# Radius-64 scores against 256 keys at once, and an output projection dealt out between the others

## What is computed

```python
proj = rms_norm(x, norm_g[0]) @ a_w_in              # 512 x 1024 by 1024 x 10240
for g, (window, dil) in enumerate(((128, 1), (512, 4), (2048, 16))):
    q, k, v = (part of proj for group g)            # 8 heads of 128
    s = q @ k.T * 128**-0.5 - slope * distance      # |distance| <= window / 2, multiples of dil
    o[g], lse[g] = softmax(s) @ v, logsumexp(s)
w = softmax(lse over g)
y = sum(w[g] * o[g]) * silu(gate)
x = x + y @ a_w_out                                 # 1024 x 1024
```

## Time and profile before

| what | value |
|---|---|
| runs | median 1941.76 us of 3 (1941.34 to 1943.03) |
| profiled execution | 1942.72 us, span 1940.9 us |
| PE busy over the span | 1800.2 us (93%) |
| DVE busy | 1084.6 us (56%) |
| ACT busy | 732.9 us (38%) |
| POOL busy | 395.7 us (20%) |
| stage A | from the start to about 1230 us |

### The profile page before, as it was taken

The page is one execution under the profiler, slowest core; times in us unless marked ns, Lnnn a source line. Parts: engine busy times, 40 slices in busy tenths (PEclk is TensorE's granted clock), DMA queues, the critical chain, the costliest instruction groups (busy, mean ns, idle before and its releaser), DMA issues. The chain is left out here.

```text
span 1940.9 us, 25427 instructions
## 1 busy us (share of the span) xinstructions
PE 1800.2 (93%) x9040; PEld 1496.7 (77%) x9040; DVE 1084.6 (56%) x1855; ACT 732.9 (38%) x1473; POOL 395.7 (20%) x319
## 2 busy tenths in 40 slices
PE   5999999999999999999999996798977999999994
PEld 4888878878888888888888886697866777777773
DVE  4344364364364364364354354735976777778785
ACT  4223223323213313313313312522136666766663
POOL 0001001001001001001001001010026666666653
PEclk9999999999999999999999998898998999999996
DMA  3111011011011011011011010201000000000002
GB/s 141 44 44 55 23 55 54 22 54 54 22 54 54 22 54 54 22 54 54 22 54 44 27 46 2 87 8 33 33 25 25 25 19 5 24 24 24 11 6 98
DMA packets 23514, 76.53 MB, mean 39 GB/s; under 512 B 3120, under 2 KB 3248, under 8 KB 22960
## 3 DMA queue, kind: packets, MB, share of 16 engines
q1 hardware_dynamic: 23472, 75.98, 11.4%
HBM read 71.77 MB, written 4.19 MB: 39 GB/s over the span
## 5 line engine op out<-in xcount | busy, mean ns | idle before, releaser
L653 PE MATMUL bankA<-hTh,wh 128*128 128x512 f32 x1280 | 505.9, 395 | 1.5 <-DVE wl L473 1.5
L653 PE MATMUL bankA<-hTh,wl 128*128 128x512 f32 x1280 | 499.6, 390 | 0.0
L653 PE MATMUL bankA<-hTl,wh 128*128 128x512 f32 x1280 | 499.0, 390 | 0.0
L653 PEld LDWEIGHTS bankA<-hTh,wh 128*128 128x128 f32 x1280 | 240.8, 188 | 53.1 <-DVE wl L473 1.9
L653 PEld LDWEIGHTS bankA<-hTh,wl 128*128 128x128 f32 x1280 | 240.7, 188 | 51.8
L653 PEld LDWEIGHTS bankA<-hTl,wh 128*128 128x128 f32 x1280 | 241.0, 188 | 48.0
L288 POOL TENSOR_TENSOR prob<-prob,wt_blk 128x1024 f32<-128x1024 f32 x16 | 37.2, 2323 | 1111.8 <-DVE wt_blk L561 1111.8
L508 DVE TENSOR_TENSOR qkl<-bankA,qkh 128x512 fp32r<-128x512 f32 x96 | 66.4, 692 | 283.7 <-ACT qkh L341 283.5
L341 ACT ACTIVATE qkh<-bankA 128x512 fp32r<-128x512 f32 x96 | 57.2, 596 | 327.1 <-PE bankA L653 325.4
L484 DVE TENSOR_TENSOR wl<-raw,wh 128x1024 fp32r<-128x1024 f32 x94 | 117.2, 1247 | 52.8 <-ACT wh L318 50.1
L318 ACT ACTIVATE wh<-raw 128x1024 fp32r<-128x1024 f32 x96 | 101.3, 1056 | 69.7 <-PE bankA L746 69.7
(11 more groups left out here) (203 smaller groups left out, 3671.7 us busy)
## 6 DMA issues: line engine op xcount, KB each, us to landing
raw<-a_w_in SPq DMA_DIRECT2D x80, 512.0 KB, 3.3
bias<-alibi SPq DMA_DIRECT2D x8, 512.0 KB, 3.7
raw<-a_w_out SPq DMA_DIRECT2D x16, 256.0 KB, 2.6
graw<-b_w_gate SPq DMA_DIRECT2D x8, 512.0 KB, 3.6
raw_o<-b_w_out SPq DMA_DIRECT2D x16, 256.0 KB, 2.8
raw_q<-b_w_q SPq DMA_DIRECT2D x8, 384.0 KB, 3.9
X<-x_prompt SPq DMA_DIRECT2D x1, 2048.0 KB, 7.8
X<-x_sample SPq DMA_DIRECT2D x1, 2048.0 KB, 11.8
```

Of the source, the lines that this page charges most:

```text
L653: ins = pe.matmul(proj_ps[b][:, :], w[a][:, slot, k * P:(k + 1) * P], hT[c][:, k, b * S:(b + 1) * S], start=(i == 0), stop=(i == last))
```

## The change

- **Scores.** A tile of 128 queries is multiplied with 256 keys in one matmul instead of with 128 keys twice: 6 matmuls of 256 columns a round instead of 12 of 128. The keys are read from the same buffer in runs of 64 elements (pair 1: tiles 0 and 3) or of 32 (pair 0: tiles 1 and 2). For tiles 0 and 3 the columns come out in another order than `prob` has them, so DVE takes those rounds with three adds: `edge_scores` (two of 128 elements) and `inner_scores` (one of 256).
- **Output rows.** The blocks `out0` and `out1` are gone. Behind each of the eight projections gate, q2, k2, v2 (b = 0, 1) PE does two rows (6 matmuls), in the two banks `out_ps`; a row waits for the add of the row two before. DVE adds a pair behind its work on the same projection.
- **Output weights.** They have buffers of their own (`raw_out`, `w_out`), are loaded at once (512 KB, behind q1's) and split once a head, behind v1 (`split_out` on ACT and DVE). Before, two splits of 1024 elements a head served them.
- **The loop.** Heads 1 and 7 are written out, the loop has heads 2 to 6. In head 7 the two splits at its end, which prepared the output weights, are left out; the last output weights are split behind `joint_softmax`. Its 16 rows still go through four banks in the same order.

```diff
--- before.py
+++ after.py
...
+ROW_SLOTS = [("gate", 0), ("gate", 1), ("q2", 0), ("q2", 1), ("k2", 0), ("k2", 1), ("v2", 0), ("v2", 1)]
+
+
+def rows_beside(name, b):
+
+    at = ROW_SLOTS.index((name, b))
+    return [(r, r // NT, r % NT) for r in (2 * at, 2 * at + 1)]
+
+
+def last_rows():
+
+    return [(2 * i + half, half, i) for i in range(NT) for half in range(2)]
+
+
+def row_no(h, r):
+    return h * OUT_ROWS - OUT_ROWS + r
 
...
+        raw_out = sb("raw_out", [P, D])
+        w_out = [sb(f"w_out{s}", [P, D], F32R) for s in "hl"]
...
+            def load_out(h):
+
+                if not (isinstance(h, int) and h == 1):
+                    sp.wait_ge(out_split, h - 1)
+                sp.dma_start(raw_out[:, :], io["a_w_out"][bass.ds(h - 1, 1)].rearrange("o p c -> (o p) c")
+                             ).then_inc(out_loaded, 16)
...
+                    if name == "q1" and not is_first(h):
+                        load_out(h)
...
+            load_block(0, "q0")
+            load_bias(0)
+            for name in PROJ[1:]:
+                load_block(0, name)
+            head(1)
+            with sp.Fori(2, A_HEADS) as h:
+                head(h)
+            load_out(A_HEADS)
...
+                k, slot = PROJ.index(name), block_slot(name)
+                act.wait_ge(raw_loaded[slot], h * 80 + 16 * (k // 2 + 1))
+
+                if not (is_first(h) and k < 2):
+                    act.wait_ge(proj_done[1], proj_no(h, name) - 1)
                 act.activation(w[HI][:, slot, :], raw[:, slot, :], ACT.Copy).then_inc(w_hi, 1)
+
+            def split_out(h):
+
+                act.wait_ge(out_loaded, h * 16)
+                if not (isinstance(h, int) and h == 1):
+                    act.wait_ge(row_done, row_no(h, 0))
+                act.activation(w_out[HI][:, :], raw_out[:, :], ACT.Copy).then_inc(out_hi, 1)
...
+                k = PROJ.index(name) + 2
+                if k < len(PROJ):
+                    split_weights(h, PROJ[k])
+                elif not (isinstance(h, int) and h == A_HEADS - 1):
+                    split_weights(h + 1, PROJ[k - len(PROJ)])
...
+                    if name == "v1" and not is_first(h):
+                        split_out(h)
...
+            def edge_scores(rows, slot):
+
+                for i, t in enumerate((0, QT - 1)):
+                    half = rows[:, t, i * P:(i + 1) * P].rearrange("p (s j w) -> p s j w", s=2, j=QT)
+                    at = 2 * P * (2 * i) + i * P
+                    add = bias[:, at:at + P].rearrange("p (s j w) -> p s j w", s=2, j=QT)
+                    ps = sum_ps[slot][:, 2 * P * i:2 * P * (i + 1)].rearrange("p (j g w) -> p g j w", g=4, w=16)
+                    dve.tensor_tensor(half, ps[:, 0:4:3], add, ALU.add)
+
+            def inner_scores(rows, slot):
+
+                dst = rows.rearrange("p t (h k) -> p (t h) k", h=2)[:, 1:7:5].rearrange("p t (j w) -> p t j w", j=QT)
+                add = bias[:, :].rearrange("p (t k) -> p t k", k=P)[:, 1:5:3].rearrange("p t (j w) -> p t j w", j=QT)
+                ps = sum_ps[slot][:].rearrange("p (t j u) -> p t j u", t=2, j=QT)[:, :, :, 16:48]
+                return dst, add, ps
...
                 if g == 0:
-                    b, pair = n // 2, n % 2
-                    dst = prob[:, 0, b, 2 * pair:2 * pair + 2, :].rearrange("p t k -> p (t k)")
-                    src = bias[:, 2 * P * pair:2 * P * pair + 4 * P]
-                    ps = sum_ps[slot][:, :]
+                    b = n // 2
+                    rows = prob[:, 0, b]
+                    if n % 2 == 0:
+                        dst = rows[:, 1:3, :]
+                        src = bias[:, 2 * P:4 * P].unsqueeze(1).broadcast_to((P, 2, 2 * P))
+                        ps = sum_ps[slot][:].rearrange("p (t k) -> p t k", t=2)
+                    else:
+                        edge_scores(rows, slot)
+                        dst, src, ps = inner_scores(rows, slot)
...
-            def add_output(h, name):
-                for k, half, n in output_rows(h, name):
-                    at = sum_no(h, "out", k)
+            def split_out(h):
+
+                dve.wait_ge(out_hi, h)
+                dve.tensor_tensor(w_out[LO][:, :], raw_out[:, :], w_out[HI][:, :], ALU.subtract).then_inc(out_split, 1)
+
+            def add_rows(h, rows, banks):
+                for r, half, n in rows:
                     cols = slice(half * HALF, (half + 1) * HALF)
-                    dve.wait_ge(sum_done, at + 1)
-                    dve.tensor_tensor(X[:, n, cols], row_ps[k % 4][:, :], X[:, n, cols], ALU.add).then_inc(sum_taken, 1)
+                    dve.wait_ge(row_done, row_no(h, r) + 1)
+                    dve.tensor_tensor(X[:, n, cols], banks[r % len(banks)][:, :], X[:, n, cols],
+                                      ALU.add).then_inc(row_taken, 1)
...
-                    for i, t in enumerate((2 * pair, 2 * pair + 1)):
-                        for half in range(2):
-                            c = t + half
-                            for m, (x, z) in enumerate(SPLIT_PRODUCT):
-                                ins = pe.matmul(ps[:, (2 * i + half) * P:(2 * i + half + 1) * P],
-                                                qk[x][:, 0, b, t * P:(t + 1) * P], key_chunk(qk[z][:, 1, b, :], c),
-                                                start=(m == 0), stop=(m == 2))
+                    for i, t in enumerate((0, 3) if pair else (1, 2)):
+                        at = 32 * t - (0, 16, 16, 32)[t]
+                        for m, (x, z) in enumerate(SPLIT_PRODUCT):
+                            keys = qk[z][:, 1, b, :].rearrange("p (j u) -> p j u", j=QT)[:, :, at:at + 64]
+                            if not pair:
+                                keys = keys.rearrange("p j (c w) -> p c j w", w=32)
+                            ins = pe.matmul(ps[:, 2 * P * i:2 * P * (i + 1)], qk[x][:, 0, b, t * P:(t + 1) * P], keys,
+                                            start=(m == 0), stop=(m == 2))
...
-            def output(h, name):
-                pe.wait_ge(w_split, block_no(h, OUTPUTS[1] if is_past(h) else name) + 1)
-                if name == "out0":
-                    pe.wait_ge(y_split, h * 2)
-                for k, half, i in output_rows(h, name):
-                    at = sum_no(h, "out", k)
-
-                    if k < 2:
-                        pe.wait_ge(sum_taken, at - 1)
-                    elif k >= 4:
-                        pe.wait_ge(sum_taken, at - 3)
+            def output(h, rows, banks):
+
+                for r, half, i in rows:
+                    if r == 0:
+                        pe.wait_ge(out_split, h)
+                        pe.wait_ge(y_split, h * 2)
+                    if r >= len(banks):
+                        pe.wait_ge(row_taken, row_no(h, r) - len(banks) + 1)
                     b, j = divmod(i, QT)
                     for m, (a, c) in enumerate(SPLIT_PRODUCT):
-                        ins = pe.matmul(row_ps[k % 4][:, :], yT[a][:, b, j * P:(j + 1) * P],
-                                        w[c][:, block_slot(h, f"out{half}"), 0:HALF], start=(m == 0), stop=(m == 2))
-                    ins.then_inc(sum_done, 1)
+                        ins = pe.matmul(banks[r % len(banks)][:, :], yT[a][:, b, j * P:(j + 1) * P],
+                                        w_out[c][:, half * HALF:(half + 1) * HALF], start=(m == 0), stop=(m == 2))
+                    ins.then_inc(row_done, 1)
...
-                        if name in PROJ:
-                            project(h, name, b)
+                        project(h, name, b)
                         if not is_first(h):
                             between(h, name, b)
+                            if (name, b) in ROW_SLOTS:
+                                output(h, rows_beside(name, b), out_ps)
...
             head(0)
-            with pe.Fori(1, A_HEADS) as h:
+            head(1)
+            with pe.Fori(2, A_HEADS - 1) as h:
                 head(h)
+            head(A_HEADS - 1)
             for name in ("q0", "k0", "v0", "q1"):
                 for b in range(NB):
                     between(A_HEADS, name, b)
-            for name in ("out0", "out1"):
-                output(A_HEADS, name)
+            output(A_HEADS, last_rows(), row_ps)
```

More of the change, by code:

```diff
@@ L81, in turn_no, with sum_slot @@
     return h * 14 + NORM_TURNS - 10 + TURNS[kind] + n
[L85 to L91, removed]
-def sum_no(h, kind, n):
[L95 to L109, removed]
+SUMS = {"s0": 0, "s1": 4, "s2": 6}
+def sum_no(h, kind, n):
+    return h * 8 + SUMS[kind] + n
+def sum_slot(kind, n):
+    return (SUMS[kind] + n) % 2
+ROW_SLOTS = [("gate", 0), ("gate", 1), ("q2", 0), ("q2", 1), ("k2", 0), ("k2", 1), ("v2", 0), ("v2", 1)]
[6 more added lines that the diff above has]
+    return h * OUT_ROWS - OUT_ROWS + r
 def turn_slot(h, kind, n):
@@ L241, in load_block @@
             def load_block(h, name):
-                n = block_no(h, name)
-                slot = block_slot(h, name)
```

(38 more changed lines are left out.)

58 lines of the change are left out of this document (21 added, 37 removed).

## The result

| | before | after |
|---|---|---|
| median of the runs | 1941.82 us (4 runs, 1941.34 to 1943.03) | 1914.86 us (4 runs, 1914.14 to 1916.11) |
| profiled execution | 1942.72 us, span 1940.9 | 1914.14 us, span 1912.3 |

The ratio is 0.986, with an interval from 0.985 to 0.987: 27.0 us faster by the medians, 28.6 by the two profiled executions (the experiment on the first 35 us shows where the other 1.6 come from). The median before has one run more than the one that the forecast started from.

A forecast was written before the change was run, and what follows sets the result against it. PE was taken to bound the attention stage, 60 to 1180 us. Scores 13.2, output block 11.6 and tail 1.0 sum to 25.8 us off the median 1941.76: 1916.0 us, range 1911 to 1925.

The forecast's parts named there:

- scores, seven heads: Radius-64 scores, every head but the first: 256-column matmuls, held by late DVE, save PE 1.60 us a head.
- scores, head 0: Radius-64 scores of the first head, where DVE is free: 3.25 us instead of 5.31, gain 2.06 us.
- output block, seven heads: Output rows moved behind projections: PE's waits for DVE's X adds vanish, 1.66 us a head, 11.6 in all.
- tail: E to PE's restart, longer by: Last head, from projections' end E: softmax starts 0.63 us earlier, but DVE's weight split makes POOL stand 1.05.
- Price of the strided 256-column matmul: Radius-64 scores on PE: 0.118 us each, like the value product; bounds 0.111 and 0.222.
- the scores would then gain nothing: Rival: in the scores the strided 256-column matmul costs 0.222 us; total gain 12.6, 1929 us; chance 0.06.
- DVE holds the scores: Radius-64 scores: PE waits for DVE to empty banks, 0.87 us before round 2, so a head gains 1.60 us.
- Margin at the gate: Gate projection: DVE adds the output rows 0.85 us or more before PE needs their banks.
- The rival that PE waits there: At the gate PE waits for X adds after all: 8 us back, 1924 us; chance 0.07.
- the slower case: Rival: each of 16 switches a head between projection and output rows drains PE's queue; 1949.6 us at 0.30 each; chance 0.02.
- The short strided adds: Rival: DVE's short adds in the scores cost like full ones, 0.61 us each; total gain about 18, 1924 us; chance 0.08.
- The ledger of 0 for the ACT and DVE splits, the transfer and the loop: Fewer splits a head, one 512 KB output-weight transfer and two heads out of the loop change PE's time by 0.

The follow-up runs named there:

- the experiment on the first 35 us: Nothing changed: the kernel before executed once more, 1941.03 us, and the changed kernel twice more, 1916.07 and 1916.39 us.
- turns_between: Changed kernel, but PE does the two turns of v0 between the second and third round of the scores: 1909.11 us, ratio to the kernel before 0.9828.
- gate_load: Changed kernel plus one unread DVE maximum over 1024 elements behind each half of the gate, ahead of its X adds: 1919.11 us, ratio 0.9877.
- late_split: Changed kernel, with DVE's split of the last output weights moved behind the tail's first two splits of turned probabilities: 1916.45 us, ratio 0.9865.

## Why the prediction was right

Forecast 1916.0 (1911 to 1925), measured 1914.86. Term by term, from the profiled executions:

| term | forecast us | measured us |
|---|---|---|
| scores, seven heads | 7 x 1.60 | 7 x 1.59 |
| scores, head 0 | 2.06 | 1.99 |
| output block, seven heads | 7 x 1.66 = 11.6 | 7 x 1.86 = 13.0 |
| tail: two rows leave PE's path | 1.39 | 1.36 |
| tail: E to PE's restart, longer by | 1.05 - 0.63 = 0.42 | 14.39 - 14.06 = 0.33 |
| sum | 25.8 | 27.2 |

- **Price of the strided 256-column matmul.** Right: 0.118 to 0.12 us, that of the contiguous one. Against the change stood the line of the Trainium skill ("Advanced Engine Details and Errata", PSUM Cachelines) that a non-contiguous pattern significantly slows matmuls. The trace doesn't agree with it: neither reading in runs of 32 nor of 64 cost anything here, and the value product writes PSUM in runs of 32 at the same 0.118. That the scores would then gain nothing was my own step; the line gives no factor.
- **DVE holds the scores.** Right, and it is the step that made the number: 24 matmuls at 0.118 alone would have given 2.55 a head. `turns_between` shows the rest to be a wait. That the sum came out to 0.01 us is luck in part: PE stood 0.74 us instead of 0.86 before round 2 and not at all before round 3, where I had 0.06, and the first matmuls behind the turn and behind the stop cost 0.19 more than reckoned.
- **The output block** is the one term that was mis-sized: 1.66 forecast, 1.86 measured in a head, 1.4 us in all. The stops were what I read. I had priced the rows at 0.228 and the pair at up to 1.39; among the projections they cost 0.227, 1.36 a pair: 0.07 a head less than I had reckoned. And I took off 0.10 for the slow first matmul behind the turns, as moved to the projection. But the six half-projections (24 matmuls each) behind the old block had paid about as much already. Before, 144 matmuls of projection follow on 696.94 until

```profile
729.75 0.22 PE L729 MATMUL bankA<-qkh 128*128 128x128 f32 x1
```

32.81 us; after, the same six take 5.58 and five times 5.44, 32.78. So nothing was added to them, and the block's whole 12.71 came down to 8 x 1.36 = 10.88.
- **Margin at the gate.** Right: I had 0.85 us or more, the trace shows 0.8, and `gate_load` found it again. The rival that PE waits there didn't happen, but it was 0.8 us away. It held that 1 to 2 us more of DVE's work would bring back 8 us; one load of 1.12 behind each half of the gate brought 4, two brought 20.
- **The tail.** Right to 0.1 us, with the collision, which `late_split` takes away: POOL's multiply lasts 1.90 again. From PE's restart to the next stage nothing changed, as forecast (38.14 and 38.11 us).
- **The rivals.** Switches between rows and projections cost nothing (no start in a pair or behind it is late), so the slower case had no ground. The short strided adds cost 0.20 each, not 0.61. The ledger of 0 for the ACT and DVE splits, the transfer and the loop holds: of the 3.49 us by which a head is shorter the scores and the output block explain 3.45.

## What to carry to other kernels

When an engine that bounds the program gets cheaper instructions, write down when the engine that empties its banks comes to them; here that ledger took more than a third off the gain in the scores (1.60 instead of 2.55 a head), and 1.59 was measured. Then give the bound engine other work in the gap: moving two groups of turns brought back 0.78 us a head, most of what the ledger had taken. And where the bound engine comes to depend on another one's queue, there is a margin that a load of known length can measure: here 0.8 us were free, and nearly all beyond it was paid.

## What the runs showed of the hardware

- A matmul of 256 fp32r columns costs 0.118 to 0.12 us whether its moving operand is contiguous or read in runs of 32 or 64, one of 128 columns 0.111.
- DVE's add follows its elements down to 128, with the source in PSUM in runs of 16: two of 128 start 0.39 us ahead of the next instruction, 0.20 each.
- After a stop PE is slow for longer than one matmul: 0.34 and then 0.23 to 0.24 instead of 0.227 for the next six to ten, so that a stop of 0.35 us cost 0.55 in the end.
- The engines don't meet only at semaphores, against what the section on the chip says: DVE's split of weights, which is released by ACT, and POOL's multiplies hold each other up. In the middle heads before, the split started 0.4 us ahead of the end of POOL's second multiply and lasted 1.52 instead of 1.23, and POOL's third lasted 2.87. After, it starts 1.3 us ahead of the end of the third, and the fourth is the long one (the POOL row shown):

```profile
595.93 2.41 DVE L495 TENSOR_TENSOR wl<-raw,wh 128x1024 fp32r<-128x1024 f32 x1 [0.26 <-ACT wh L318]
```

```profile
597.21 2.88 POOL L293 TENSOR_TENSOR prob<-prob,wt 128x1024 f32<-128x1024 f32 x1
```

DVE's split waits out POOL's third multiply (2.41 us instead of 1.23), and POOL's fourth then waits for the split (2.88 instead of 1.90). I had not reckoned with it; PE has no idle time there, so it cost nothing. The two sides take turns, a whole instruction at a time, as the exclusive lock of the Trainium skill ("SBUF — State Buffer", Who interferes with whom) says.
- The clock granted between 24 and 31 us is 0.50 (1.2 GHz) in some executions and 1.00 (2.4 GHz) in others of the same kernel. PE had started at 17 us and paused twice, for 1.0 to 2.2 us, in either case. The first projection then takes from 5.58 to 7.40 us, and 7.83 in `late_split`, whose row reads 1.00.
